# Neighbourhood attention on row and column tiles, with every copy of the second head's turned probabilities on ACT

## The reference

```python
def na_context(h, P, o):                       # 128 context tokens
    q, k, v = [split_heads(t, b, s) for t in jnp.split(h @ P['na_w_qkv'][o], 3, axis=-1)]
    y = dense_context_attention(q, k, v)       # softmax(q k^T / 8) v over the 128 context keys
    return y @ P['na_w_out'][o], k, v          # k and v are outputs

def na_latent(h, P, o, k_ctx, v_ctx):          # 512 latent tokens, cached context keys and values
    s_loc = jnp.einsum('brjqhd,brjkhd->brjhqk', qb, k_loc) * scale + bias   # 8 rows x 32 columns: 256 keys
    s_ctx = jnp.einsum('brjqhd,bshd->brjhqs', qb, k_ctx) * scale            # 128 keys
    p = jax.nn.softmax(jnp.concatenate([s_loc, s_ctx], axis=-1), axis=-1)
    out = (jnp.einsum('brjhqk,brjkhd->brjqhd', p[..., :n_loc], v_loc)
           + jnp.einsum('brjhqs,bshd->brjqhd', p[..., n_loc:], v_ctx))
    return out.reshape(b, l, NA_INNER) @ P['na_w_out'][o]
```

## Time and profile before

| | |
|---|---|
| median of 3 runs | 2008.21 us (2008.07 to 2008.69) |
| the profiled execution's own time | 2007.91 us |
| its span in the trace | 2006.2 us |
| PE busy (matmul) | 1929.6 us, 96% |
| DVE, ACT, POOL busy | 1021.0, 685.4, 632.7 us |
| chain that ended last, by engine | PE 32%, DVE 1%, DMA 1% of the span (the rest is not followed) |
| mean granted TensorE clock | 0.98 |

### The profile page before, as it was taken

The page is one execution under the profiler, slowest core; times in us unless marked ns, Lnnn a source line. Parts: engine busy times, 40 slices in busy tenths (PEclk is TensorE's granted clock), DMA queues, the critical chain, the costliest instruction groups (busy, mean ns, idle before and its releaser), DMA issues. The chain is left out here.

```text
span 2006.2 us, 36105 instructions
## 1 busy us (share of the span) xinstructions
PE 1929.6 (96%) x13465; PEld 1862.9 (93%) x13465; DVE 1021.0 (51%) x1986; ACT 685.4 (34%) x1045; POOL 632.7 (32%) x309
## 2 busy tenths in 40 slices
PE   5998999999999999999999989989999999999997
PEld 3997888888899999999999979989999999999997
DVE  5646666776623555314554344556546554135543
ACT  4442222232422443312334321147624443223333
POOL 1232222222232333343335422333132333433342
PEclk8999999999999999999999999999999999999999
DMA  8224454445443222222222522211141222222221
GB/s 322 64 88 142 132 161 131 135 158 162 163 135 105 63 73 71 71 79 78 70 62 67 164 60 64 74 40 26 33 137 53 84 65 66 78 84 73 61 66 72
DMA packets 272871, 192.30 MB, mean 96 GB/s; under 512 B 25370, under 2 KB 259222, under 8 KB 271270
## 3 DMA queue, kind: packets, MB, share of 16 engines
q1 hardware_dynamic: 267638, 182.81, 29.9%
q10 hardware_dynamic: 5168, 8.59, 1.2%
HBM read 181.31 MB, written 10.06 MB: 95 GB/s over the span
## 5 line engine op out<-in xcount | busy, mean ns | idle before, releaser
L543 POOL TENSOR_TENSOR w_lo<-raw,w_hi 128x1024 fp32r<-128x1024 f32 x244 | 594.4, 2439 | 1270.5 <-ACT w_hi L1070 1270.5
L599 PE MATMUL ps<-act_hi,w_hi 128*128 128x322 f32 x2752 | 847.7, 315 | 6.8 <-DVE act_lo L1577 2.6
L600 PE MATMUL ps<-act_lo,w_hi 128*128 128x322 f32 x2624 | 803.3, 312 | 0.0
L603 PE MATMUL ps<-act_hi,w_lo 128*128 128x322 f32 x2752 | 635.6, 312 | 0.0
L599 PEld LDWEIGHTS ps<-act_hi,w_hi 128*128 128x128 f32 x2752 | 525.7, 191 | 22.0 <-issue 14.1
L600 PEld LDWEIGHTS ps<-act_lo,w_hi 128*128 128x128 f32 x2624 | 498.8, 190 | 0.0
L603 PEld LDWEIGHTS ps<-act_hi,w_lo 128*128 128x128 f32 x2752 | 466.0, 189 | 0.0
L1070 ACT ACTIVATE w_hi<-raw 128x1024 fp32r<-128x1024 f32 x244 | 256.2, 1051 | 392.5 <-PE ps L603 353.7
L599 PE MATMUL ps<-f_hi,w_hi 128*128 128x322 f32 x704 | 214.2, 311 | 0.0
L600 PE MATMUL ps<-f_lo,w_hi 128*128 128x322 f32 x704 | 213.7, 310 | 0.0
L1859 DVE SCALAR_TENSOR_TENSOR x<-ps,mod,x 128x128 f32 (+1 forms) x144 | 54.4, 433 | 264.9 <-PE ps L603 264.3
(11 more groups left out here) (298 smaller groups left out, 2098.8 us busy)
## 6 DMA issues: line engine op xcount, KB each, us to landing
ada<-in_ada_w SPq DMA_DIRECT2D x40, 1024.0 KB, 5.3
raw<-in_ssd_w_in SPq DMA_DIRECT2D x44, 512.0 KB, 3.8
raw<-in_ffn_w_gate SPq DMA_DIRECT2D x44, 512.0 KB, 3.7
raw<-in_ffn_w_up SPq DMA_DIRECT2D x44, 512.0 KB, 3.7
raw<-in_ffn_w_down SPq DMA_DIRECT2D x32, 384.0 KB, 3.4
raw<-in_na_w_qkv SPq DMA_DIRECT2D x24, 512.0 KB, 3.8
raw<-in_ffn_w_down SPq DMA_DIRECT2D x32, 320.0 KB, 3.2
first<-in_ada_w SPq DMA_DIRECT2D x8, 1024.0 KB, 13.2
```

Source lines behind the costliest of these rows:

```text
L543: g.tensor_tensor(w_lo[:, s], raw[:, s % RAW], w_hi[:, s], ALU.subtract).then_inc(S["low_split"], 1)
L599: t.matmul(out, hi, chunk_of(src_hi, k0 + k, cols), start=start, stop=False)
L600: t.matmul(out, hi, chunk_of(src_lo, k0 + k, cols), start=False, stop=False)
L603: mm = t.matmul(ps[:, 2 * tset + h, 0:HALF], lo, chunk_of(src_hi, k0 + k, cols), start=False, stop=stop)
```

## The change

In V, each turning of a tile now stands behind one more projection tile, and the turning of the last tile and of the cached keys stand behind the first two K tiles. The context keys of all pairs are turned together during Q, and DVE copies them to `kc` there. DVE writes the scaled queries straight into block order, so `queries`, `qz` and its memset go.

In attention, both heads of a block are worked together. Scores use 64-partition matmuls straight from `kt` and `qt`, one on each half of the partitions (row tiles), into three PSUM banks in turn. Values use `vtok` columns as weights (64 of them) and stream the 128 probabilities, one head into PSUM partitions 0 to 63, the other into 64 to 127 (column tiles), so outputs come out channel-major and `turn_outputs` goes. In its place the inverse sums are spread over the partitions by matmuls (`spread_rows`), copied by ACT (`spread_copy`) and multiplied in by DVE (`scaled_out`). Of the two copies of turned probabilities per block, DVE makes the first head's and ACT the second head's, in all 40 blocks (`ON_ACT`). The loops are unrolled, the exponential is written in place, and the 80 small memsets of `sums` become one. The first output tile waits chunk by chunk for `act_lo` rather than for the last pair.

```diff
-            v_windows(0, 3)
             for s in range(4):
                 whole_tile(SLOT_QKV, 1, s, TILE_QKV, 4, s)
-                if s > 0:
-                    v_windows(1, s - 1)
-            v_windows(1, 3)
+                v_windows((3 + s) // 4, (3 + s) % 4)
+            for part, i in ((1, 0), (1, 1), (2, 0), (2, 1)):
+                for s in range(4):
+                    whole_tile(SLOT_QKV + part * C, i, s, TILE_QKV + part * C, 4, s)
+                    if (part, i, s) == (1, 0, 0):
+                        v_windows(1, 3)
...
+            def scores(n):
...
+                if n > 0:
+                    pe.wait_ge(S["scores_taken"], 2 * n - 1)
...
+                    for h in range(2):
+                        hp = slice(64 * h, 64 * h + 64)
...
+                        t.matmul(ps[:, (2 * n + h) % 3, 0:256], qt[hp, i * TQ + b * P:i * TQ + b * P + P], grid, start=True, stop=True)
+                for h in range(2):
+                    hp = slice(64 * h, 64 * h + 64)
+                    keys = kct[hp, i * P:i * P + P] if b < LC else kt[hp, i * TQ + NLAT:i * TQ + TQ]
+                    mm = t.matmul(ps[:, (2 * n + h) % 3, 256:384], qt[hp, i * TQ + b * P:i * TQ + b * P + P], keys, start=True, stop=True)
...
+            def values(n):
...
+                for k in range(3) if b < LC else [2]:
+                    for h in range(2):
+                        cols = slice(i * P + 64 * h, i * P + 64 * h + 64)
+                        lhs = vtok[:, 7, cols] if b == LC else vc[:, cols] if k == 2 else vtok[:, WIN[b] // 8 + 2 * k, cols]
+                        out = ps[64 * h:64 * h + 64, 5 if b < LC else 7, b % LC * P:b % LC * P + P]
+                        mm = t.matmul(out, lhs, ptb[:, n % 2, h, k * P:k * P + P], start=(k == 0 or b == LC), stop=(k == 2))
...
+            for n in range(BLOCKS + 3):
+                if n < BLOCKS:
+                    scores(n)
+                if 2 <= n < BLOCKS + 2:
+                    values(n - 2)
+                if n >= NC and n % NC < 2:
+                    spread_rows(n // NC - 1, n % NC)
+                if 1 <= n < BLOCKS + 1:
+                    turn(n - 1)
...
+                    whole_tile(SLOT_NA + 4 * part, 0, s, TILE_NA + 4 * part, 4, s, frees=4 * part + s == C - 1,
+                               before=("o_low", 1) if part == 0 and s == 0 else None)
```

ACT's and DVE's loops over blocks:

```diff
+            for n in range(BLOCKS + NC):
+                i, b = n // NC - 1, n % NC
+                if n < BLOCKS:
+                    probs(n, 0)
+                    probs(n, 1)
+                if 1 <= n <= BLOCKS:
+                    turned_copy(n - 1)
+                if i >= 0 and b < 2:
+                    spread_copy(i, b)
+                if i >= 0 and b == 3:
+                    outputs_high(i)
...
+            for n in range(BLOCKS + NC):
+                i, b = n // NC - 1, n % NC
+                if n < BLOCKS:
+                    scored(n, 0)
+                    scored(n, 1)
+                if i >= 0 and 1 <= b < 3:
+                    scaled_out(i, b - 1)
+                if 1 <= n <= BLOCKS:
+                    turned_copy(n - 1)
```

More of the change, by code:

```diff
@@ L329, in trunk, with copied @@
         DEFERRED = {2: (3, 4, R_NFFN), 3: (MODS, MODS + 1, R_NMIX + C), 4: (MODS + 3, MODS + 4, R_NFFN + C)}
+        BLOCKS = C * NC
+        ON_ACT = [True for n in range(BLOCKS)]
+        def copied(n, h):
+            if h == 1 and ON_ACT[n]:
+                return "pt_copied_act", sum(ON_ACT[:n + 1])
+            return "pt_copied_dve", n + 1 + sum(not q for q in ON_ACT[:n + (h == 1)])
         block = ctx.enter_context(nc.Block())
@@ L990, in scores @@
[L990 to L1008, removed]
-                    mm = t.matmul(out, ptb[:, u % 2, 256:384], vc[:, cols], start=False, stop=True)
-                else:
-                    mm = t.matmul(out, ptb[:, u % 2, 256:384], vtok[:, 7, cols], start=True, stop=True)
-                mm.then_inc(S["o_ready"], 1)
@@ L1014, in turn_outputs @@
-            def turn_outputs(i):
-                pe.wait_ge(S["o_taken"], 2 * i + 4)
-                pe.wait_ge(S["o_low"], i + 1)
-                for n in range(LC):
-                    t.transpose(ps[:, 6, n * P:n * P + P], ot[:, n, :], ident[:])
-                t.transpose(ps[:, 7, P:2 * P], kx, ident[:])
-                t.transpose(ps[:, 7, 0:P], ot[:, LC, :], ident[:]).then_inc(S["o_transposed"], 1)
-            def step(i, u, last=None):
-                scores(i, u)
-                for lag, work in ((2, turn), (3, values)):
-                    if u >= lag:
-                        work(i, u - lag)
-                    elif last is not None:
-                        work(last, u - lag + UNITS)
@@ new lines, in spread_rows @@
+            def spread_rows(i, ctx):
+                pe.wait_ge(S["sums_inverted"], 2 * i + ctx + 1)
+                if ctx:
+                    blocks = [LC]
+                    if i >= 1:
+                        pe.wait_ge(S["sums_copied"], 2 * i)
+                else:
+                    blocks = range(LC)
+                    if i >= 1:
+                        pe.wait_ge(S["sums_copied"], 2 * i - 1)
+                    else:
+                        pe.wait_ge(S["keys_out"], 1)
+                for b in blocks:
+                    for h in range(2):
+                        out = ps[64 * h:64 * h + 64, 7 if ctx else 6, P if ctx else b * P:2 * P if ctx else b * P + P]
+                        mm = t.matmul(out, rsum[:, i % 2, b, h:h + 1].broadcast_to([P, 64]), ident[:], start=True, stop=True)
+                mm.then_inc(S["sums_spread"], 1)
@@ L2068, in _ @@
[L2068 to L2082 removed]
+                tt(act_lo[:, cx], ao[:, NLAT:TQ], act_hi[:, cx], ALU.subtract).then_inc(S["o_low"], 1)
```

315 lines of the change are left out of this document (143 added, 172 removed).

## The result

| | before | change |
|---|---|---|
| median, same chip, 4 runs each | 2008.14 us (2005.84 to 2008.69) | 1974.84 us (1973.71 to 1977.16) |
| the profiled execution's own time | 2007.91 us | 1977.16 us |
| its span | 2006.2 us | 1975.4 us |
| PE, DVE, ACT busy | 1929.6, 1021.0, 685.4 us | 1906.4, 1011.7, 672.3 us |

The ratio of the two kernels is 0.984, with a 95% interval of 0.9828 to 0.9852: 33.3 us faster by the medians, 30.8 by the two profiled executions. On another chip, in the last group of experiments, the same two kernels had medians of 2007.13 and 1977.67, 29.5 apart. The forecast was 29.6 less, 1978.3.

What follows compares the result with a forecast made beforehand. PE was taken to bound attention, waiting for other engines in V and at attention's start and end. 15.8 - 0.9 + 14.7 = 29.6 us less than 2007.9 gave 1978.3 us, range 1970 to 1993.

Steps and rivals of the forecast that it cites:

- V and the turnings: V: moved turnings leave tiles 8.0 us apart, 15.8 us less; turning context keys in Q adds 0.9.
- a pair: Attention loop: a pair of heads takes 13.0 us instead of about 14.94, with PE still the bound.
- Row tiles: Attention scores on PE: both heads' matmuls run side by side, 0.65 us per latent block, or 1.30 if not.
- rival 2: Attention scores: row tiles do not pair, 15.4 us per pair, 1996 us in all; chance 0.12.
- Switches: Attention on PE: three changes of array shape per block cost 0.15, 0.20 and 0.20 us, 2.75 per pair.
- The wait that takes the place: Attention loop: values wait for ACT's copy, 2.59 us after scores; 0.3 shows twice per pair, 0.65.
- Rival 1: Attention loop: ACT becomes the bound, an exponential occupying 0.60 + 0.19; 13.7 us per pair, 1984 in all; chance 0.15.
- Start: Start of attention: bias holds the first scores, block 2 starts 10.1 us behind Q tile 7; half clock costs 1.4.
- End: End of attention: third output tile waits 2.3 us for `x`, 16.6 behind PE's end; 14.7 less in all.
- rival 4: Attention: granted clock stays at 0.50 throughout, 22 us per pair, 2047 in all, slower; chance 0.06.

Runs made afterwards that it cites:

- V alone: The kernel before with only PE's order in V and K as in the change: 1990.53 us, ratio 0.9926.
- the extra pair: The change plus a one-column matmul with 64-column weights between the two heads' transposes in each block: 1986.87 us, ratio 0.9904.
- the stores early: The change with ACT issuing the stores of new keys and values in block 2 of attention: 1973.62 us, ratio 0.9831.
- all three: The change with bias built earlier, last queries scaled in block 2, stores in block 2, and ACT's copy between the exponentials: 1964.08 us, ratio 0.9783.

## Why the prediction was right

Both medians of the change, 1974.8 and 1977.7, lie 3.5 and 0.6 us under the forecast of 1978.3 and inside its range of 1970 to 1993. The second lies as near as it does by luck, since the two are 2.8 apart. What counts more is that the terms hold one by one, with two misses at the end that cancel. By the profiled executions:

| step | forecast | trace |
|---|---|---|
| V and the turnings, V tile to Q tile 7 | 15.8 less, 0.9 back | 14.96 less |
| block 2's scores behind Q tile 7 | 10.1 | 9.92 |
| a pair | 13.0 | 12.88 |
| waits in the loop per pair | 0.65 | 0.62 |
| PE's end behind Q tile 7 | 113.8 | 112.8 |
| third output tile behind it | 16.6 | 17.5 |
| third output tile behind Q tile 7 | 130.4, 14.7 less | 130.27, 14.81 less |
| behind that tile | nothing | 1.4 less |
| ahead of the V tile | nothing | 0.4 more |

- **V**: the order of PE's program cost what the steps of the earlier trace rows showed beyond 8.02, and the lower clock in the earlier trace rows was part of that. V alone measured it by itself.
- **Row tiles**: the one fact that no row showed. 0.65 was taken from L847's column tiles, and 1.30 kept as a bound. The rows of the change fit 0.65, and both heads on one half of the rows brought 0.96 for what takes 0.53: rival 2 was priced right, and did not happen.
- **Switches**: 0.15, 0.20 and 0.20 were read off two places in the earlier trace rows. A block measures 0.85 + 0.81 + 0.80 = 2.46 against 0.65 + 0.65 + 0.66 + 0.55 = 2.51, so three switches took 0.50, and the extra pair of them 0.36 against 0.35.
- **The wait that takes the place**: from the end of a block's scores to values behind both exponentials and the copy, 2.59 was summed up from single rows. In the change the scores issued at 1334.54 end at 1334.54 + 0.39 - 0.165 = 1334.77, and the values start at 1337.40: 2.63. The forecast had two waits of 0.3 per pair; they were one of 0.44 and one of 0.18. Rival 1 fell with it. It asked for an exponential that occupies 0.79 when another follows; in ACT's timeline of the change the second exponential starts 0.60 behind the first, and the reading of the row sum lies within it:

```profile
1316.29 0.60 ACT L1387 ACTIVATE sp<-sp,nmax 128x384 f32<-128x384 f32 x1
...
1316.80 0.19 ACT L1387 ACTIVATION_READ_ACCUMULATOR sp<-sp,nmax 128x1 f32 x1
1316.89 0.60 ACT L1387 ACTIVATE sp<-sp,nmax 128x384 f32<-128x384 f32 x1
```

- **Start**: that the bias would hold it was right: DVE's first score stands at 1313.13, 1.4 behind the last queries, and with bias and queries out of the way block 2 comes 5.8 us sooner. The low clock was expected to last to 13 behind Q tile 7 and to cost 1.4; it ended at 12.9 and cost 1.1 from block 2 to block 5.
- **End**: PE was 1.0 sooner, about what eight pairs of 12.88 instead of 13.0 make, and the chain behind it 0.9 longer. The reload started 4.8 behind PE's end instead of 4.5, and it took 9.91 instead of the 9.30 of the earlier trace rows. The wait for `x` was 3.0 instead of 2.3. These are two misses of one size that cancel, and the sum owes part of its closeness to that.
- **Clock through attention (rival 4)**: the granted clock is 1.00 from 1320.30 on, with PE busy 94% of it. Transposes are 0.80 of a block's 2.46 us, a third of the stream. The Trainium skill (TensorE: Matmul & The Clock Gate, Part 4) says that transposes do not count as activity. A clock that fell for it does not show in the trace, at this share of transposes.

What the forecast left out is the 1.4 us behind the third tile, where the code is the same. The 75 us from that tile on have a mean granted clock of 0.95 in the kernel before, 0.98 in the change and 0.96 in the change's second profile:

```profile
1467.00:1542.00 75.00, 73.24 (x475) 72.97 (x476) 44.12 (x77) 30.11 (x45) 23.19 (x10) 0.95 0.22 64
```

```profile
1437.60:1512.60 75.00, 73.24 (x485) 72.99 (x486) 45.61 (x78) 31.65 (x47) 24.73 (x10) 0.98 0.22 64
```

```profile
1436.70:1511.70 75.00, 73.24 (x478) 72.97 (x479) 44.52 (x77) 30.52 (x46) 23.63 (x10) 0.96 0.22 64
```

From the third tile to the end they take 539.2, 537.8 and 539.5 us. The order fits, and the second profile of the same code has the longer time back: the 1.4 is scatter, not gain. A part of this scatter has its place at the third output tile itself. Eight profiled executions have PE wait about 3 us for `x` there. In six of them the clock falls there, as in the change's second profile, whose first matmul takes 0.61 instead of 0.39; in the change's first it stayed up. With a wait of about 1 us (0.9 with the stores early, 1.0 with all three) it stayed up in both.

```profile
1436.67 0.61 PE L607 MATMUL ps<-act_hi,w_hi 128*128 128x322 f32 x1 [3.07 <-DVE x L1878]
```

**What stays open.** Why the low clock starts between 2.7 and 5.5 us behind Q tile 7 in kernels in which PE's program there is the same, so that the time from block 2 to block 5 is 8.6 to 10.1 us, was not tried, nor why it lasts 6.8 us in one of them (the stores early) and 10.2 in the others. Nor was whether the reload of `x` would be quicker than 9.9 us if the loads of weights that are issued 0.4 us behind it stood elsewhere.

## What to carry to other kernels

Before pairing narrow matmuls on row or column tiles, count the changes of shape per step: here they took 0.50 of a block's 2.46 us, could be read in advance from two places in another part of the kernel, and left a gain since two 64-wide matmuls then cost one. When a faster stream takes a wait away at a seam, look for the next thing that is late and for the clock: here PE's wait of 6.3 us for the queries' copy gave way to one of 5.7 for the bias, and once bias and last queries were both out of the way, the clock stayed up as well. Two edits that each gain a microsecond or two are told by the same marks in both traces (a pair, the last tile behind a fixed tile), not by medians that scatter as much, and least by medians from different chips.

## What the runs showed that was not expected

- No row of the kernel before had shown it: float32 matmuls of 64 rows on the two halves of the array's rows run side by side, 0.53 us for two heads' 256 columns against 0.96 on one half.
- A matmul of one column cost PE 0.36 us where its shape differed from both neighbours, which is more than three transposes of 128 columns (0.32).
- The clock at the seam stayed up once PE's wait there was short: 7.04 us of work in 12.90 came with a mean of 0.60, 10.76 in 12.90 with 1.00. At the third output tile the same wait of 3 us came with a fall in some executions and with none in others.
- One kernel's profiled executions on two chips differ by 0.5 us between Q tile 7 and the third output tile (130.27 and 130.80); 0.4 of it lies between blocks 2 and 5, at the lower clock. Ahead of the V tile from which this document counts, the same code took 1153.2 to 1157.6 us in the profiled executions of the kernels made from the change, more than most of the edits are worth.
